# Expert stage: token rows gathered as quarter rows and turned by VectorE, gate and up weights loaded in the matching row order

## The chip, the cores and the metric

The kernel runs on one core of one Trainium2 chip. The metric is the device time in microseconds (us) of one execution. A comparison of two kernels is the ratio of their times.

## The reference

One layer of a decoder block over 1024 tokens of width 1024: a normalised input projection, two attention mixers, a gated merge, an output projection, and then a sparse expert layer. The change touches only the expert layer and the tables that it reads. Cut to that part:

```python
def moe_ffn(h, router_w, router_b, w_gate_up, b_gate_up, w_down, b_down):
    logits = (xf @ router_w + router_b)
    top_logit, top_idx = lax.top_k(logits, TOP_K)          # 4 of 32 experts for each token
    gate = jax.nn.softmax(top_logit, axis=-1)
    ...
    def expert_block(args):                                # x_blk: the rows of one expert
        x_blk, e = args
        gu = x_blk @ w_gate_up[e] + b_gate_up[e]           # 1024 -> 2048
        g = jnp.minimum(gu[:, :D_FF], SWIGLU_LIMIT)
        u = jnp.clip(gu[:, D_FF:], -SWIGLU_LIMIT, SWIGLU_LIMIT)
        act = (u + 1.0) * (g * jax.nn.sigmoid(SWIGLU_ALPHA * g))
        return act @ w_down[e] + b_down[e]                 # 1024 -> 1024
    ...
    out = out.at[buf_token].add(yb * buf_gate[:, None])
```

An expert has 8 MB (8.39 million bytes) of gate and up weights and 4 MB (4.19 million bytes) of down weights in float32, and there are 32 experts.

## The kernel before

The front part (to about 822 us) does the norm, the attention, the merge, the output projection and the routing. Then `experts` runs one block for each of the 32 experts. A block holds up to 160 token rows (`CAP`): 128 rows in the main part, which every block computes, and 32 more (`CAP2`) in the "rest" part, which PE computes only for an expert with more than 128 tokens. Of the 32 blocks 18 have the rest part.

**Weights.** An expert's weights are 12 slabs of 1 MB (128 partitions x 2048 floats, tile `raw`, called `ex_raw` in the profile). Slabs 0 to 7 are gate and up (`load_gate_up`, L1360), slabs 8 to 11 are down (L1988). Each slab comes in two loads of 512 KB, all issued in order by SyncE (SP). The slot of slab i is loaded for the next expert as soon as PE has used it (`raw_mm`), so loads run up to twelve slabs ahead. The biases come in four loads of three rows of 6144 bytes each (L2004). The first four slabs of expert 0 are loaded during routing, from `output_and_route`; the rest of them wait in the program for the first gathered rows (`x_in`).

**Splitting.** For each slab ACT writes a rounded copy `w_hi` (`split_hi`, L2027), DVE the remainder `w_lo` (`split_lo`, L2302), and PE multiplies three times: x_hi by w_hi, x_lo by w_hi, x_hi by w_lo (`gate_up` L2433, `down` L2477). The rest part multiplies the 32 further rows by the raw slab (L2455, L2494).

**Token rows.** GpSimd (POOL) gathers the 128 main rows of the next block but one into `xg` in one indirect DMA of 4 KB rows, and the further 32 rows as quarter rows (piece q of row r stands on partition 32q + r) into `xg2` in a second one (L2137, L2140). PE turns them with ten 128x128 transposes in `turn_x` (L2385), into the PSUM tiles `gu` and `tr`; ACT copies them to `x_hi` and `x_rest` (L2066), DVE writes `x_lo` (L2343). In the program of PE `turn_x(b + 1)` stands in block b between `turn_hidden(b, 1)` (L2393), which turns the second half of the hidden activations, and the down slab 10, whose first matmul waits for ACT's copy `h_hi` of what `turn_hidden(b, 1)` wrote.

**Activation.** For each half ACT writes sigmoid(1.702 g) (L2033), and DVE does three steps: clamp of up (L2312), gate times sigmoid (L2315), minimum and product (L2317). The rest part does the same on 256 columns (L2039, L2325 to L2328).

**Order.** Everything is written out by hand: each engine's order is the order of the code, and engines wait for one another by counting semaphores. SP's queue is in program order. Before the routing it writes `rt_blank` (59 rows of 1280 bytes) to `slots` (L1447) and two tiles of zeros (128 rows of 2560 bytes each) to `xn_s` (L1452). At the end of routing it issues four loads of gate and up weights for expert 0 and then the last store of `xn_s` (the normalised rows, L1467), on which the first gather of the expert stage waits.

Of the kernel before, what the change touches and what calls it, by code (L numbers as in the profile page):

```python
# [21 lines left out]
P = 128  # L22
T = 1024
# [22 lines left out]
NBLK = NE + MAXOVER  # L46

# [1323 lines left out]
def output_and_route(nc, x, w_out, ffn_norm_w, router_w, router_b, ident, nhalf, mT_hi, mT_lo, raw,  # L1371
                     raw_in, wo_hi, wo_lo, out, xn_s, slots, rt, w_gate_up, slab_raw, slab_in, acc, xn_last):
    with ExitStack() as ctx:
# [36 lines left out]
        place, spare_row, quarter = rt["place"], rt["spare_row"], rt["quarter"]  # L1410
        which = rt["which"].rearrange("p (t j) -> p t j", j=TOPK)
# [20 lines left out]
        with nc.Block() as block:  # L1432
# [41 lines left out]
            def _(act):  # L1474
# [49 lines left out]
                act.preload_act_table_set("sigmoid_and_others")  # L1524
# [4 lines left out]
            def _(pool):  # L1529
# [44 lines left out]
                for g in range(Q):  # L1574
# [5 lines left out]
                                        .to_broadcast([P, KD, NE]), ALU.mult).then_inc(c_set, 1)  # L1580
                each = lambda b: b.rearrange("p (j o) -> p j o", o=1).to_broadcast([P, TOPK, NE])
# [294 lines left out]
def experts(nc, xn_s, w_gate_up, w_down, ident, rt, slots, bp_s, out, raw, w_in_, xn_last):  # L1876
# [5 lines left out]
    with ExitStack() as ctx:  # L1882
# [12 lines left out]
        over_n, cum, base1 = (sb(f"ex_{n}", [P, NE]) for n in ("over", "cum", "base1"))  # L1895
        home, low, destf = (sb(f"ex_{n}", [P, NT * TOPK]) for n in ("home", "low", "destf"))
# [4 lines left out]
        idx2 = sb("ex_idx2", [P, 1], U32)  # L1901
# [5 lines left out]
        xg = sb("ex_xg", [P, D])  # L1907
        xg2 = sb("ex_xg2", [P, XW])
# [5 lines left out]
        hid = sb("ex_hid", [P, FF])  # L1914
        hid2 = sb("ex_hid2", [P, 2, P])
# [22 lines left out]
        x_tr, xh_d, xl_d = sem("e_x_tr"), sem("e_xh"), sem("e_xl")  # L1938
        y_ev, y2_ev = sem("e_y_ev"), sem("e_y2_ev")
        idx_in, idx2_d, x_in, y_out = sem("idx_in"), sem("idx2_d"), sem("x_in"), sem("e_y_out")  # L1940
# [36 lines left out]

        block = ctx.enter_context(nc.Block())

        @block.sync  # L1980
        def _(sp):
# [25 lines left out]
            sp.wait_ge(x_in, 32)  # L2007
# [12 lines left out]
        def _(act):  # L2020
# [8 lines left out]
            def sigmoid(b, half):  # L2029
# [5 lines left out]
            def sigmoid_rest(b):  # L2035
# [4 lines left out]
                                     ACT.Sigmoid, scale=ALPHA).then_inc(sg2_d, 1)  # L2040
# [13 lines left out]
            def take_x(b):  # L2054

                if not isinstance(b, int) or b > 0:
                    act.wait_ge(slab_mm, SLABS * (b - 1) + 8 + RING)
                    act.wait_ge(raw_mm, SLABS * (b - 1) + 8)
                for g in range(3):
                    act.wait_ge(x_tr, 3 * b + g + 1)  # L2060
                    if g < 2:
                        dst, src = x_hi[:, 4 * g:4 * g + 4, :], gu[:, 0, g, :].rearrange("p (k c) -> p k c", k=4)
                    else:
                        dst = x_rest[:, :, :].rearrange("p (q h) c -> p h q c", h=2)
                        src = tr[:, 0:2 * P].rearrange("p (h q c) -> p h q c", h=2, q=Q)
                    nc.scalar.activation(dst, src, ACT.Copy).then_inc(xh_d, 1)  # L2066
# [20 lines left out]
            def body(b, over, first=False):  # L2087
# [5 lines left out]
                sigmoid(b, 0)  # L2093
# [5 lines left out]
                sigmoid(b, 1)  # L2099
                sigmoid_rest(b)  # L2100
# [15 lines left out]
        def _(pool):  # L2116
# [14 lines left out]
            def rows():  # L2131

                nc.gpsimd.tensor_scalar(idx2[:, :], nxt[:, 1, 0:1].bitcast(U32), float(Q), quarter[:, 0:1],
# [493 lines left out]
```

## Time and profile before

| | us |
|---|---|
| three runs of the kernel | 2211.8, 2210.14, 2206.59 (median 2210.14) |
| span of the profiled execution | 2210.2 |
| expert stage, from the first instructions to the end | 822 to 2210 |
| a block without the rest part | 35.4 |
| a block with the rest part | 47.5 |

The profile is one execution of the program, and its span is taken as that execution's own time; it is equal to the median of the runs to 0.1 us. Times inside it are us from the start of the span. PE is TensorE's matmuls, PEld its weight loads, DVE VectorE, ACT ScalarE, POOL GpSimd, SP SyncE. There are 16 DMA engines; a DMA share of 1 means that all 16 had a packet under way all the time, and packets that overlap on an engine can bring it above 1.

### The profile page before, as it was taken

The page shows a single profiled execution, that of the slowest core. Times are in us where ns is not written, and L with a number is a line of the kernel's source. Part 1 is how long each engine was busy: PE and PEld are TensorE (multiplying, and loading weights), DVE is VectorE, ACT ScalarE, POOL GpSimd, SP SyncE. Part 2 cuts the span into 40 slices and gives each one's busy share as a digit, 9 for nine tenths or more (in the row PEclk, how much of TensorE's full clock was granted, in tenths as well). Part 3 has the DMA queues.
Part 4 walks back from the last instruction along what each step waited for, and adds up shares of the span by engine and source line. Part 5 has one row for each costly group of instructions (what it writes and reads, how often), then busy time and mean ns, then how long its engine had stood idle before and what let it go on. Part 6 is the DMA issues. An engine that isn't in the chain of part 4 may idle for free.

```text
span 2210.2 us, 39028 instructions
## 1 busy us (share of the span) xinstructions
PE 2131.3 (96%) x13778; PEld 1656.0 (75%) x13779; DVE 1612.0 (73%) x1575; ACT 1323.9 (60%) x1496; POOL 595.1 (27%) x556
## 2 busy tenths in 40 slices
PE   7989999999999978999999999999999999999997
PEld 7867777777777766777777777777887777777775
DVE  4165767676576456888888887898997778777787
ACT  4266666757453225576676675676876566665665
POOL 1120101010075342153354431232341222222222
PEclk9999999999999988999999999999999999999998
DMA  4101212111266539899999998999998889888993
GB/s 153 37 22 47 68 35 70 36 58 59 82 193 198 185 126 334 296 326 340 312 349 340 317 345 291 357 351 343 396 370 318 292 310 321 306 305 267 332 320 117
DMA packets 267125, 515.15 MB, mean 233 GB/s; under 512 B 34821, under 2 KB 77264, under 8 KB 267052
## 3 DMA queue, kind: packets, MB, share of 16 engines
q1 hardware_dynamic: 243052, 471.90, 59.5%
q0 software_dynamic: 17088, 39.14, 7.1%
q10 hardware_dynamic: 6912, 3.15, 0.5%
q8 instruction: 44, 0.72, 0.1%
q14 instruction: 29, 0.24, 0.0%
HBM read 475.82 MB, written 42.45 MB: 234 GB/s over the span
## 4 chain that ended last, share of the span: by engine, by line
PE 58%; SPq 1%; issue 1%; DMA 1%; DVE 1%; ACT 0%; POOL 0%; ACTq 0%; POOLq 0%; DVEq 0%
PE ex_gu L2433 30%; PE ex_yp L2477 15%; PE ex_rest L2455 6%; PE ex_rest L2494 3%; PE ex_gu L2385 1%; SPq L1360 1%; PE ex_tr L2393 1%; PE ex_gu L2393 1%; DMA ex_bias<-bp_s 1%; PE ex_gu L2420 0%; DVE ex_wlo L2302 0%; ACT ex_whi L2027 0%; PE ex_tr L2385 0%; PE ex_yp L2424 0%; PE ex_rest L2449 0%
## 5 line engine op out<-in xcount | busy, mean ns | idle before, releaser
L2302 DVE TENSOR_TENSOR ex_wlo<-ex_raw,ex_whi 128x2048 fp32r<-128x2048 f32 x387 | 873.7, 2289 | 197.5 <-ACT ex_whi L2027 178.0
L2027 ACT ACTIVATE ex_whi<-ex_raw 128x2048 fp32r<-128x2048 f32 x387 | 733.6, 1927 | 181.0 <-PE ex_gu L2433 132.8
L2433 PE MATMUL ex_gu<-ex_whi,ex_xhi 128*128 128x512 f32 x1024 | 284.3, 399 | 5.2 <-issue 5.2
L2433 PE MATMUL ex_gu<-ex_whi,ex_xlo 128*128 128x512 f32 x1024 | 275.0, 390 | 0.0
L2433 PE MATMUL ex_gu<-ex_wlo,ex_xhi 128*128 128x512 f32 x1024 | 274.7, 390 | 0.0
L2433 PEld LDWEIGHTS ex_gu<-ex_whi,ex_xhi 128*128 128x128 f32 x1024 | 186.4, 188 | 61.2 <-issue 26.2
L2433 PEld LDWEIGHTS ex_gu<-ex_whi,ex_xlo 128*128 128x128 f32 x1024 | 192.8, 188 | 41.1
L2433 PEld LDWEIGHTS ex_gu<-ex_wlo,ex_xhi 128*128 128x128 f32 x1024 | 192.8, 188 | 40.8
L57 PE MATMUL at_job<-xnT_hi,at_whi 128*128 128x512 f32 x416 | 179.6, 432 | 5.2 <-DVE at_nxt_qa L777 2.8
L59 PE MATMUL at_job<-xnT_hi,at_wlo 128*128 128x512 f32 x416 | 165.1, 397 | 0.0
L58 PE MATMUL at_job<-xnT_lo,at_whi 128*128 128x512 f32 x416 | 164.6, 396 | 0.0
L741 POOL TENSOR_TENSOR at_wlo<-at_raw,at_whi 128x1024 fp32r<-128x1024 f32 x15 | 36.1, 2405 | 452.1 <-ACT at_whi L554 452.1
L2137 POOL DMA_INDIRECT ex_xg<-xn_s,ex_nxt x33 | 33.8, 1025 | 430.6 <-PE ex_tr L2385 428.8
L2147 POOL DMA_INDIRECT out_dram<-ex_ytok,ex_cur x32 | 68.2, 2132 | 295.5 <-issue 224.7
L2477 PE MATMUL ex_yp<-ex_whi,ex_hhi 128*128 128x512 f32 x512 | 144.8, 404 | 0.0
L2477 PE MATMUL ex_yp<-ex_whi,ex_hlo 128*128 128x512 f32 x512 | 137.5, 390 | 1.2 <-DVE ex_hlo L2335 1.2
L2477 PE MATMUL ex_yp<-ex_wlo,ex_hhi 128*128 128x512 f32 x512 | 137.3, 390 | 0.0
L2455 PE MATMUL ex_rest<-ex_raw,ex_xrest 128*32 128x256 f32 x2304 | 135.7, 381 | 0.0
L2477 PEld LDWEIGHTS ex_yp<-ex_whi,ex_hhi 128*128 128x128 f32 x512 | 90.9, 188 | 30.1 <-issue 7.4
L2477 PEld LDWEIGHTS ex_yp<-ex_whi,ex_hlo 128*128 128x128 f32 x512 | 96.0, 188 | 22.5 <-DVE ex_hlo L2335 1.6
L2477 PEld LDWEIGHTS ex_yp<-ex_wlo,ex_hhi 128*128 128x128 f32 x512 | 96.1, 188 | 20.8
L2455 PEld LDWEIGHTS ex_rest<-ex_raw,ex_xrest 128*32 128x32 f32 x2304 | 70.4, 110 | 53.3 <-issue 12.7
(381 smaller groups left out, 3631.6 us busy)
## 6 DMA issues: line engine op xcount, KB each, us to landing
ex_raw<-in_w_gate_up_dram SPq DMA_DIRECT2D x512, 512.0 KB
ex_raw<-in_w_down_dram SPq DMA_DIRECT2D x256, 512.0 KB
at_raw<-in_w_in_dram SPq DMA_DIRECT2D x25, 512.0 KB
gT<-at_gst SPq DMA_DIRECT2D x32, 256.0 KB, 2.3
mg_g<-gT SPq DMA_DIRECT2D x32, 256.0 KB, 3.8
raw_o<-in_w_out_dram SPq DMA_DIRECT2D x8, 512.0 KB, 5.9
op_x<-in_x_dram SPq DMA_DIRECT2D x8, 512.0 KB, 4.1
out_dram<-op_h SPq DMA_DIRECT2D x8, 512.0 KB, 2.9
```

Source lines behind the costliest of these rows:

```text
L57: nc.tensor.matmul(out, w_hi, x_hi, start=first, stop=False)
L58: nc.tensor.matmul(out, w_hi, x_lo, start=False, stop=False)
L59: return nc.tensor.matmul(out, w_lo, x_hi, start=False, stop=last)
L741: nc.gpsimd.tensor_tensor(w_lo[:, s, :, :], raw[:, s, :, :], w_hi[:, s, :, :].bitcast(F32), ALU.subtract).then_inc(wlo_d, 1)
L2027: nc.scalar.activation(w_hi[:, i % RING, :], raw[:, i % SLABS, :], ACT.Copy).then_inc(hi_d, 1)
L2147: pool.indirect_dma_start(out=out[0, :, :], out_offset=bass.IndirectOffsetOnAxis(ap=cur[:, 0, 0:1].bitcast(U32), axis=0), in_=ytok[:, :], ...
L2302: nc.vector.tensor_tensor(w_lo[:, slot, :], raw[:, i % SLABS, :], w_hi[:, slot, :].bitcast(F32), ALU.subtract).then_inc(lo_d, 1)
L2393: last = nc.tensor.transpose(dst[:, k * P:(k + 1) * P], hid[:, (4 * half + k) * P:(4 * half + k + 1) * P], ident[:, :])
L2433: mm = nc.tensor.matmul(gu[:, half, h, :], x[:, k, :], w[:, kk, h, :], start=half == 0 and k == 0 and n == 0, stop=k == KD - 1 and n == 2)
L2455: mm = nc.tensor.matmul(part(g), x_rest[:, k, :], gate_up_slab(raw, i)[:, kk, :, g * P:(g + 1) * P], start=k == 0, stop=k == KD - 1)
L2477: mm = nc.tensor.matmul(yp[:, nh, :], x[:, k, :], w[:, kk, nh * HALF:(nh + 1) * HALF], start=False, stop=k == KD - 1 and n == 2)
L2494: mm = nc.tensor.matmul(part(g), h_rest[:, k, :], down_slab(raw, i)[:, kk, g * XW:(g + 1) * XW], start=k == 0, stop=k == KD - 1)
```

## The change

**Gather.** `xg` becomes 128 partitions x 5 pieces of 256 floats. Piece a (0 to 4) is gathered by an indirect DMA of its own: quarter rows of the 32 tokens in slots 32a to 32a + 31, with quarter q of token r on partition 32q + r. The row numbers for on-chip blocks are made once before the first block (`rows_of`, by seven more small DVE steps and sixteen small matmuls).

**Turn.** DVE transposes 32x32 blocks (`turn_x`, `turn_x_rest`: two of 128x512 and one of 128x256 per block) from `xg` into `x_t`, which lies in the tile `hid`, and into `x_rest`. ACT's copy to `x_hi` and DVE's `x_lo` read `x_t` in place of PSUM; ACT's copy to `x_rest` goes. PE's `turn_x` is gone.

**Weights' rows.** With this layout partition 32q + r of K tile k holds input channel 256q + 32k + r, where before it was 128k + p. So `load_gate_up` reads the rows of the weights in that order: the source's outermost count is the quarter q (4), then r (32), then the halves and 512 contiguous floats. The destination is as before: 128 partitions, each two runs of 512 floats. The down loads are unchanged.

**Activation.** ACT's function is now gate times sigmoid(1.702 gate) in one (`Gelu_apprx_sigmoid`), so that DVE's L2315 and L2326 go.

```diff
+NQ = CAP // CAP2
...
-    gate_up_v = w_gate_up.rearrange("a e (k p) (h c) -> (a e) p k h c", p=P, h=2)
+    gate_up_v = w_gate_up.rearrange("a e (q k r) (h c) -> (a e) q r k h c", q=Q, k=KD, h=2)
     half, pair_of_k = divmod(i, 4)
     for kk in range(2):
         sp.dma_start(raw[:, i, :].rearrange("p (k h c) -> p k h c", k=2, h=2)[:, kk, :, :],
-                     gate_up_v[bass.ds(e, 1), :, 2 * pair_of_k + kk, :, half * HALF:(half + 1) * HALF]
-                     .rearrange("a p h c -> (a p) h c")).then_inc(raw_in[i], 16)
+                     gate_up_v[bass.ds(e, 1), :, :, 2 * pair_of_k + kk, :, half * HALF:(half + 1) * HALF]
+                     .rearrange("a q r h c -> (a q) r h c")).then_inc(raw_in[i], 16)
...
-                nc.scalar.activation(sg[:, :], gu[:, half, 0, :], ACT.Sigmoid, scale=ALPHA).then_inc(sg_d, 1)
+                nc.scalar.activation(sg[:, :], gu[:, half, 0, :], ACT.Gelu_apprx_sigmoid).then_inc(sg_d, 1)
...
+            def gather(table):
+                for a in range(NQ):
+                    pool.indirect_dma_start(out=xg[:, a, :], out_offset=None, in_=xn_s.rearrange("t (q c) -> (t q) c", q=Q),
+                                            in_offset=bass.IndirectOffsetOnAxis(ap=table(a), axis=0)).then_inc(x_in, 16)
...
-                nc.vector.tensor_tensor(sg[:, :], gu[:, half, 0, :], sg[:, :], ALU.mult).then_inc(part_d, 1)
...
+            def turn_x(b, g):
+
+                if g == 0:
+                    dve.wait_ge(x_in, 16 * NQ * (b + 1))
+                after(dve, h_tr, 3 * b + g - 2)
+                mine = slice(4 * g, 4 * g + 4)
+                nc.vector.transpose(x_t[:, mine, :].rearrange("p k (a c) -> p k a c", a=Q),
+                                    pieces[:, mine, 0:Q, :]).then_inc(x_tr, 1)
...
                 split_lo(b, 11)
+                turn_x(b + 1, 0)
+                turn_x_rest(b + 1)
                 hidden_lo(b, 1)
+                turn_x(b + 1, 1)
                 take_x(b + 1)
...
                 turn_hidden(b, 1, alone=not more)
                 if more:
                     turn_hidden_rest(b)
-                turn_x(b + 1)
                 main(10)
```

The order of PE's instructions in a block, between the down slabs 9 and 10, of the kernel before (`ex_hid` is the hidden tile, `ex_hhi` ACT's copy of its turned form, `e_hh` the count of those copies):

```order
L2477 MATMUL ex_yp<-ex_wlo,ex_hhi 128x512 x3
L2393 MATMUL ex_gu<-ident,ex_hid 128x128 [waits e_hid]
L2393 MATMUL ex_gu<-ident,ex_hid 128x128 x3
L2380 ISA
L2385 MATMUL ex_gu<-ident,ex_xg 128x128 [waits x_in]
L2385 MATMUL ex_gu<-ident,ex_xg 128x128 x7
L2385 MATMUL ex_tr<-ident,ex_xg 128x128 x2
L2463 REGISTER_ALU
L2467 REGISTER_ALU [waits e_hi]
L2477 MATMUL ex_yp<-ex_whi,ex_hhi 128x512 [waits e_hh]
```

The same place in the changed kernel:

```order
L2494 MATMUL ex_yp<-ex_wlo,ex_hhi 128x512 x3
L2410 MATMUL ex_gu<-ident,ex_hid 128x128 [waits e_hid]
L2410 MATMUL ex_gu<-ident,ex_hid 128x128 x3
L2480 REGISTER_ALU
L2484 REGISTER_ALU [waits e_hi]
L2494 MATMUL ex_yp<-ex_whi,ex_hhi 128x512 [waits e_hh]
```

The ten transposes of token rows are gone, so the matmul that waits for ACT's copy stands right behind the transposes that the copy reads.

The order of SP's instructions from the end of routing into the expert stage, which is the same in both kernels but for line numbers, here of the changed one (`op_mm` counts the output projection, `op_xn_d` the normalised rows):

```order
L1361 DMA ex_raw<-in_w_gate_up_dram 128x2x512 [waits op_mm]
L1361 DMA ex_raw<-in_w_gate_up_dram 128x2x512 x3
L1469 DMA xn_s<-op_xn 128x1024 [waits op_xn_d]
L1434 UNCONDITIONAL_BRANCH [waits op_xn_out1,op_h_out1,rt_zout,op_xn_out0,op_h_out0]
L1990 UNCONDITIONAL_BRANCH [waits barrier_Pool_Activation_PE_DVE_SP_release]
L1361 DMA ex_raw<-in_w_gate_up_dram 128x2x512 [waits x_in]
L1361 DMA ex_raw<-in_w_gate_up_dram 128x2x512
L2014 DMA ex_bias<-bp_s 3x3072 [waits e_ones]
```

No instruction moved in this piece; four of the reordered loads stand ahead of the last store of `xn_s`.

## Rows read from the trace of the kernel before

**Rows 1.** The page: DMA busy share in 40 equal slices of the span.

```profile
DMA  4101212111266539899999998999998889888993
```

**Rows 2.** The page: the chain that ended last, by line.

```profile
PE ex_gu L2433 30%; PE ex_yp L2477 15%; PE ex_rest L2455 6%; PE ex_rest L2494 3%; PE ex_gu L2385 1%; SPq L1360 1%; PE ex_tr L2393 1%; PE ex_gu L2393 1%; DMA ex_bias<-bp_s 1%; PE ex_gu L2420 0%; DVE ex_wlo L2302 0%; ACT ex_whi L2027 0%; PE ex_tr L2385 0%; PE ex_yp L2424 0%; PE ex_rest L2449 0%
```

**Rows 3.** Windows, one block with rest, one without: busy by engine, clock, DMA share.

```profile
1471.30:1518.70 47.40, 47.40 (x375) 35.12 (x374) 38.45 (x27) 29.25 (x25) 8.49 (x9) 1.00 0.87 300
1436.00:1471.00 35.00, 35.00 (x168) 28.59 (x167) 33.50 (x25) 27.12 (x24) 13.59 (x9) 1.00 1.04 392
```

**Rows 4.** DMA queues, 837 to 2140 us: packets, MB, share of 16 engines.

```profile
q1 hardware_dynamic: 170535, 390.75, 81.5%
q0 software_dynamic: 15776, 36.15, 11.1%
```

**Rows 5.** DMA, 1438 to 1447 us, inside a block without rest.

```profile
DMA packets 1289, 3.71 MB, mean 412 GB/s; under 512 B 145, under 2 KB 145, under 8 KB 1289
```

**Rows 6.** DMA issues, whole span: KB each.

```profile
ex_raw<-in_w_gate_up_dram SPq DMA_DIRECT2D x512, 512.0 KB
ex_raw<-in_w_down_dram SPq DMA_DIRECT2D x256, 512.0 KB
...
ex_bias<-bp_s SPq DMA_DIRECT2D x128, 18.0 KB
...
slots<-rt_blank SPq DMA_DIRECT2D x1, 73.8 KB
```

**Rows 7.** SP timeline: a store of 59 rows, then two of 128 (start, us).

```profile
717.25 0.29 SPq L1447 DMA_DIRECT2D slots<-rt_blank  x1
717.58 0.81 SPq L1452 DMA_DIRECT2D xn_s<-rt_zeros  x2
```

**Rows 8.** DMA, 716 to 724 us: GB/s in 40 slices of 0.2 us.

```profile
GB/s 138 82 21 3 1 1 1 1 1 2 1 27 263 320 320 326 307 358 320 358 192 128 166 134 102 77 26 26 26 26 26 26 26 26 26 26 0 0 0 0
```

**Rows 9.** DMA, 721.70 to 723.10 us, in the tail of rows 8.

```profile
DMA packets 15, 0.04 MB, mean 26 GB/s; under 512 B 1, under 2 KB 1, under 8 KB 15
```

**Rows 10.** SP timeline, end of routing (start, us, what).

```profile
811.80 2.61 SPq L1360 DMA_DIRECT2D ex_raw<-in_w_gate_up_dram  x4
821.02 0.33 SPq L1467 DMA_DIRECT2D xn_s<-op_xn  x1
829.77 1.21 SPq L1360 DMA_DIRECT2D ex_raw<-in_w_gate_up_dram  x2
```

**Rows 11.** POOL timeline: first gather of the stage.

```profile
824.51 1.25 POOL L2178 DMA_INDIRECT ex_xg<-xn_s,ex_tab  x1 [6.79 <-DVE ex_tab L2248]
```

**Rows 12.** Timeline, end: last matmuls of the program.

```profile
2194.28 1.07 PE L2477 MATMUL ex_yp<-ex_wlo,ex_hhi 128*128 128x512 f32 x4
```

**Rows 13.** PE timeline, four equal matmuls behind idle time, and later.

```profile
841.03 1.71 PE L2433 MATMUL ex_gu<-ex_wlo,ex_xhi 128*128 128x512 f32 x4
...
847.15 1.07 PE L2433 MATMUL ex_gu<-ex_wlo,ex_xhi 128*128 128x512 f32 x4
```

**Rows 14.** Timeline, block without rest: PE's turns and ACT's copy.

```profile
1464.27 0.60 PE L2393 MATMUL ex_gu<-ident,ex_hid 128*128 128x128 f32 x4
1464.70 1.04 PE L2385 MATMUL ex_gu<-ident,ex_xg 128*128 128x128 f32 x8
1464.90 0.60 ACT L2046 ACTIVATE ex_hhi<-ex_gu 128x512 fp32r<-128x512 f32 x1 [3.12 <-PE ex_gu L2393]
...
1465.72 1.18 PE L2477 MATMUL ex_yp<-ex_whi,ex_hhi 128*128 128x512 f32 x4
```

**Rows 15.** The same place in a block with rest.

```profile
1508.23 0.60 ACT L2046 ACTIVATE ex_hhi<-ex_gu 128x512 fp32r<-128x512 f32 x1 [3.92 <-PE ex_gu L2393]
1508.25 1.04 PE L2385 MATMUL ex_gu<-ident,ex_xg 128*128 128x128 f32 x8
...
1509.26 1.17 PE L2477 MATMUL ex_yp<-ex_whi,ex_hhi 128*128 128x512 f32 x4
```

**Rows 16.** Groups of DVE's instructions, 850 to 2210 us: busy us, mean ns.

```profile
L2315 DVE TENSOR_TENSOR ex_sg<-ex_gu,ex_sg 128x512 f32<-128x512 f32 x64 | 43.5, 680 | 0.0
```

More of the change, by code:

```diff
@@ L2057, in take_x @@
                     act.wait_ge(slab_mm, SLABS * (b - 1) + 8 + RING)
[L2058 to L2066, printed above, removed]
+                for g in range(2):
+                    mine = slice(4 * g, 4 * g + 4)
+                    act.wait_ge(x_tr, 2 * b + g + 1)
+                    nc.scalar.activation(x_hi[:, mine, :], x_t[:, mine, :], ACT.Copy).then_inc(xh_d, 1)
             def take_y(b):
@@ L2092, in body @@
                     split_hi(b, i)
-                sigmoid(b, 0)
+                swish(b, 0)
                 split_hi(b, 7)
@@ L2166, in next_rows @@
                     load_slots(b)
-                    hold(pool, idx_in, 16 * (1 + Q) * (b - NE + 1), spare)
-                rows()
-                hold(pool, idx2_d, b + 1, spare)
-                if not isinstance(b, int) or b > 0:
-                    hold(pool, x_tr, 3 * b, spare)
-                gather()
+                    hold(pool, idx_in, 16 * (1 + Q * (1 + NQ)) * (b - NE + 1), spare)
+                    nc.gpsimd.tensor_scalar(idx[:, :], nxt_q[:, :, 0].bitcast(U32), float(Q), quarter[:, 0:1],
+                                            ALU.mult, ALU.add).then_inc(idx_d, 1)
+                hold(pool, idx_d, b, spare)
+                hold(pool, x_tr, 2 * b, spare)
+                hold(pool, xr_tr, b, spare)
+                gather(lambda a: idx[:, a:a + 1])
             def first_rows():
@@ L2314, in activate @@
                 dve.wait_ge(sg_d, n + 1)
-                nc.vector.tensor_tensor(sg[:, :], gu[:, half, 0, :], sg[:, :], ALU.mult).then_inc(part_d, 1)
-                dve.wait_ge(part_d, 6 * b + 2 * half + 2)
+                dve.wait_ge(part_d, 3 * b + half + 1)
                 nc.vector.scalar_tensor_tensor(out=us, in0=sg[:, :], scalar=SWISH_CAP, in1=us, op0=ALU.min, op1=ALU.mult).then_inc(hid_d, 1)
             def activate_rest(b):
-                gate, up = (rest[:, :].rearrange("p (a h c) -> p a h c", a=2, h=2)[:, :, h, :] for h in range(2))
+                up = rest[:, :].rearrange("p (a h c) -> p a h c", a=2, h=2)[:, :, 1, :]
                 dve.wait_ge(sg2_d, b + 1)
@@ L2376, in _ @@
             pe.sem_inc(slab_mm, RING)
-            def turn_x(b):
-                pe.wait_ge(x_in, 32 * b + 32)
-                for g in range(3):
-                    dst = gu[:, 0, g, :] if g < 2 else tr[:, :]
-                    for k in range(4 if g < 2 else 2):
-                        src = xg[:, (4 * g + k) * P:(4 * g + k + 1) * P] if g < 2 else xg2[:, k * P:(k + 1) * P]
-                        last = nc.tensor.transpose(dst[:, k * P:(k + 1) * P], src, ident[:, :])
-                    last.then_inc(x_tr, 1)
             def turn_hidden(b, half, alone=False):
@@ L2528, in _ @@
             for h in range(2):
-                last = nc.tensor.matmul(tr[:, 2 * NE * h:2 * NE * (h + 1)], rt["table"][:, h * P:(h + 1) * P],
-                                        rt["pair_sum"][:, :], start=True, stop=True)
+                nc.tensor.matmul(tr[:, 6 * NE * h:6 * NE * h + 2 * NE], rt["table"][:, h * P:(h + 1) * P],
+                                 rt["pair_sum"][:, :], start=True, stop=True)
+            for a in range(Q):
+                for q in range(Q):
+                    last = nc.tensor.matmul(turned_q[q * CAP2:(q + 1) * CAP2, a, :], rt["table"][:, a * CAP2:(a + 1) * CAP2],
+                                            rt["pair_sum"][:, 0:NE], start=True, stop=True)
             last.then_inc(t_tr, 1)
-            pe.wait_ge(tab_d, 2)
-            turn_x(0)
             def body(b, over):
```

106 lines of the change are left out of this document (61 added, 45 removed).

## The prediction

> **What bounds the kernel now.** I read the page's chain of work first. In the expert stage it is PE nearly throughout: the gate and up matmuls, the down matmuls and the two rest products hold 54% of the span, of the 63% that the stage takes [rows 2]. The windows of single blocks say the same: 35.00 of 35.00 us busy without rest, 47.40 of 47.40 with it, at the full clock (1.00 is 2.4 GHz) [rows 3]. Two others stand close behind. DVE is busy 33.50 of 35.00 us, and the DMA engines have a share of 1.04, that is, no free time in a block without rest; a block with rest leaves them some (0.87) [rows 3]. Over the stage the 16 engines are near their limit in every slice [rows 1], and when they are full they move 412 GB/s [rows 5], which is 25.8 GB/s for one engine. So the kernel stands on two legs: PE's work, and all 16 DMA engines carrying the weights at once. The change takes a little from the first and touches the second.
>
> **The loads of weights, the part that decides.** Bytes, descriptors and destination stay the same, the order of the source's rows does not: the source's outermost count was a run of 128 partitions' rows and is now 4 quarters. The question is over how many of the 16 engines such a transfer is spread. The trace has one transfer that answers half of it. SP issues at 717.25 a store of 59 rows of 1280 bytes (73.8 KB), and behind it two stores of 128 rows [rows 6, 7]. The two spread: the rate is about 320 to 358 GB/s. But then the core moves 26 GB/s and nothing else from 721.2 to 723.2 [rows 8], in packets that come one at a time: 15 in 1.40 us [rows 9]. 26 GB/s is one engine's share of 412. So the 59 rows were all on one engine (59 x 1280 B at 25.8 GB/s is 2.9 us), and what that engine owed of the two stores behind them (2 x 8 rows of 2560 B, 1.6 us) came late. 59 has no divisor up to 16 but 1, while 128 rows go to 16. That is what an even division of the outermost count gives. A source whose outermost count is 4 can be divided so by 4 at most, although the destination has 128. I take it that the reordered loads run on 4 engines. No row shows a transfer whose two sides differ in this way, so this is an inference and keeps a chance against it.
>
> The Trainium skill ("DMA: Bandwidth & Descriptors", section "Why a DMA increments its semaphore by 16 and not by 1") states the same rule outright: the number of engines is the largest up to 16 that divides the slowest dimension of both sides, and on the queue that SP uses it is the lowest-numbered ones. The 59 rows agree with it. By that rule these loads all share the same four engines; with a spread over 16 the sum would be that of the first rival.
>
> Do successive loads take the same four? After the 59 rows the zeros' share on that engine waited, which shows only that an engine's queue is in order. Were the fours rotated, the load would even out and the slowdown vanish; that is part of the first rival.
>
> **The sum for four engines.** What one of the four has to do for one block:
> - Gate and up: 16 loads of 512 KB (512 loads for 32 blocks) [rows 6] are 8.39 MB, a quarter of it 2.10 MB, at 25.8 GB/s 81.3 us.
> - Down: 8 loads, 4.19 MB over 16 engines, 0.262 MB: 10.2 us.
> - Biases: four loads of 18 KB [rows 6] over three engines: 24.6 KB each, 1.0 us.
> - Gathers and stores of POOL's queue: 11.1% of the engines' time from 837 to 2140 [rows 4], 145 us over 30.9 blocks of 42.2 us, 4.7 us. The gathers become five of 128 KB where they were one of 512 KB and one of 128 KB, the same bytes; I leave the term as it is.
>
> Sum 97.2 us for each block, against 35.4 to 47.5 now. It is not hidden: the prefetch is one block deep, and demand exceeds supply in every block. Of block 0 eight of the sixteen gate and up loads were made in routing, so the stage has 31.5 x 81.3 + 32 x 15.9 = 3070 us of work for these four engines.
>
> The start: four loads issued at 811.80 keep them busy 4 x 131 KB / 25.8 GB/s = 20.3 us each, until 833. The last store of `xn_s` stands behind them (issued at 821.02), and the first gather, which runs at 824.51 now, waits for it [rows 10, 11]: about 835. Its rows arrive 5.3 us later (829.77 is where SP goes on now), so streaming begins at 840. The four loads of slabs 0 and 1, early in routing, are done long before they are needed; they delay the loads and stores of routing that are issued behind them by up to 20 us once, which its double buffers mostly cover; I count nothing, at most 15.
>
> The end: behind the last landing stand the split and product of a last slab and perhaps the rest, some 8 us; from the last matmul to the end it is 2210.2 - 2195.4 = 14.9 us [rows 12]. Together 23.
>
> 840 + 3070 + 23 = 3933 us. I add 27 for unevenness (a load that waits because its slot is freed late) and say **3960**.
>
> PE cannot become the bound again, even if its clock falls for want of work. Behind idle time four matmuls take 1.71 us where the same four take 1.07 later [rows 13]. If all of PE's work took twice as long (1.2 against 2.4 GHz), a block with rest would need 95 us, still under 97, and one without 71.
>
> Bounds. Low: if POOL's packets and the weights' overlap as the share of 1.04 suggests, 3070 becomes 2950 and the time 3813. High: over the whole stage the weights' queue moved 390.75 MB in 81.5% of 1303 us on 16 engines [rows 4], 23.0 GB/s for one; all terms at that rate give 31.5 x 91.2 + 32 x 17.2 = 3423 and 4290. So 3780 to 4300.
>
> **The other edits.** They would matter only if the loads were spread over 16.
> - PE's ten transposes start at 1464.70 and the matmul behind them at 1465.72: 1.02 us; with rest 1.01 us [rows 14, 15]. But that matmul needs ACT's copy, which ends at 1465.50, or 1508.83 with rest, and then a weight load (some 0.2 us). Without the transposes PE would wait for ACT until about 1465.7 and 1509.05. The gain is 0 and 0.2 us, 18 x 0.2 = 4 us in all, where adding up transposes gives 33.
> - DVE loses two products of 0.68 us [rows 16] and one of half the columns, and gains transposes of the same three sizes. The trace has no transpose on DVE; from nothing (hidden) to twice a product's time the change per block is -1.8 to +1.8 us. At the pace of the products, the nearest row, it is 0.
> - ACT loses the copy to `x_rest`, off the path; its function costs one pass as before. POOL issues five gathers where it issued two, at some 1.3 us each [rows 11], and has 8.49 to 13.59 us of work in a block [rows 3]. The small steps ahead of block 0 and three more gather issues delay the start by some 3 us.
>
> **The rivals.**
> - *The loads spread over 16 engines after all* (the division looks at the destination only, or the fours rotate), and PE's removed transposes turn into the wait for ACT: 2210 - 4 + 3 to 2210 - 8: 2202 to 2209. For it: the destination's count is 128 and unchanged, and the trace's one odd transfer has 59 on both sides. This is the case that is not slower; it decides as soon as a load gets 16 engines, or if four engines carried over 270 GB/s. 0.11.
> - *Spread, and the transposes come back in full*: 33 x 1.0 us, 2177. Against it the end of ACT's copy [rows 14, 15]. 0.03.
> - *Spread, but a small loss*: a share of 1.04 [rows 3] has no room for more and smaller gather packets, or DVE's transposes cost double and it needs 33.5 + 1.8 = 35.3 us of a block's 35.4. One us for each of 14 blocks without rest and some at the start: 2225 (2216 to 2260). 0.06.
> - *Four engines*: 0.80.
>
> **How the numbers follow.** 0.2% (4 us) is about what a measurement of this kernel can tell from no change. Faster 0.03 and 0.07 of the first rival: 0.10; same 0.04; slower 0.86. The range 3780 to 4300 is that of the likeliest case and leaves out the 0.20 of the others.
>
> **What the profile would show.** Right: mean rate in the stage near 135 GB/s, a DMA share of 0.25 to 0.4; ACT's `split_hi` waits for loads of `ex_raw` and leads the chain; the stage takes about 3100 us, a block 97 whether it has rest or not; PE about 40% busy; the first gather near 835. Wrong: a DMA share near 1 and blocks of 35 us, which would mean that the loads were spread.

## The result and the profile after

The changed kernel takes 4310.31 us (median of 4 runs, 4304.81 to 4316.56), the kernel before 2210.7 us on the same chip; the ratio is 1.951 (95% interval 1.948 to 1.954). Forecast were 3960 us and a range of 3780 to 4300: slower, by the way that was named, and 350 us more than said, 10 us above the range.

The page of the changed kernel, its slices of DMA share and rate, and the queue from which the weights come (packets, MB, share of 16 engines), with the same queue of the kernel before last:

```profile
DMA  3121245343444344444434444443344433444443
GB/s 93 31 60 50 63 124 185 113 132 125 130 127 130 127 129 127 129 126 129 127 125 132 129 127 129 129 131 130 124 128 126 131 123 124 127 127 125 130 126 96
q1 hardware_dynamic: 236908, 471.88, 33.5%
...
q1 hardware_dynamic: 243052, 471.90, 59.5%
```

Where the share was 0.8 to 0.9 [rows 1] it is 0.3 to 0.4, with the same megabytes. The count of packets says over how many engines a load goes, since each engine that takes part ends its share with a packet of 4 bytes (from 2110 to 2120 us, where only gate and up run, there are 485 packets of 2048 bytes, about two loads, and 8 of 4 bytes). The kernel before has 243052 packets in this queue, the changed one 236908. The difference, 6144, is 512 loads times 12: 16 engines before, 4 after.

Windows of the changed kernel: two blocks with rest, one without, and the stretch in which the down loads start (busy by engine, clock, DMA share, GB/s).

```profile
2092.20:2202.10 109.90, 49.78 (x368) 35.78 (x370) 35.07 (x25) 27.98 (x22) 14.32 (x12) 0.72 0.40 126
2202.10:2312.70 110.60, 49.42 (x366) 35.65 (x367) 35.05 (x25) 27.97 (x22) 14.35 (x12) 0.72 0.40 126
2312.70:2418.20 105.50, 39.56 (x158) 30.51 (x158) 34.74 (x25) 28.00 (x22) 15.32 (x12) 0.68 0.41 131
2184.00:2198.00 14.00, 0.00 (x0) 0.00 (x0) 1.92 (x1) 0.00 (x0) 0.00 (x0) 0.50 1.03 243
```

A block takes 105.5 to 110.6 us instead of 35.0 to 47.4 [rows 3]; PE is busy in less than half of it, and more than half of its time is at the lower of its two clock levels (0.50 where it stands idle, 1.2 GHz; 0.68 to 0.72 in the mean of a block). Within a block the rate changes with what is being loaded. DMA from 2110 to 2170, 40 slices of 1.5 us:

```profile
GB/s 100 98 98 100 101 100 98 98 100 101 100 98 161 94 146 108 160 171 152 96 101 100 98 98 102 98 100 98 100 210 238 82 57 87 102 102 98 102 100 98
```

Where only gate and up weights run it is 98 to 101 GB/s, near four times the 25.8 of one engine [rows 5]. The bumps are GpSimd's gathers and stores, which use the idle engines too. The waits of the whole program that matter (us, times, longest), and SP's queue over two blocks:

```profile
PE ex_gu L2437 <- DMA ex_bias<-bp_s: 1839.8, 32, 61.5
ACT ex_whi L2037 <- DMA ex_raw<-in_w_gate_up_dram: 1435.4, 171, 13.4
...
SPq L1361 <- PE ex_rest L2472: 262.7, 17, 17.7
```

```profile
2099.78 78.35 SPq L1361 DMA_DIRECT2D ex_raw<-in_w_gate_up_dram  x16
2178.42 5.45 SPq L1998 DMA_DIRECT2D ex_raw<-in_w_down_dram  x2
2184.24 1.61 SPq L2014 DMA_DIRECT2D ex_bias<-bp_s  x4
2186.03 6.99 SPq L1998 DMA_DIRECT2D ex_raw<-in_w_down_dram  x6
2209.35 79.04 SPq L1361 DMA_DIRECT2D ex_raw<-in_w_gate_up_dram  x16
...
2296.75 6.79 SPq L1998 DMA_DIRECT2D ex_raw<-in_w_down_dram  x6
2304.21 17.36 SPq L1361 DMA_DIRECT2D ex_raw<-in_w_gate_up_dram  x3
```

One row was not in the forecast. PE's largest wait is not for weights but for the biases, at slab 3 of each block: their loads are issued behind all sixteen gate and up loads (2184.24) and land at 2202. In a block with the rest part the products of the further rows with slabs 0 to 3 stand behind slab 3, so only then does PE free these slabs, and SP issues nothing from 2193.0 to 2209.35. From 2204 to 2209 the core moves 76 GB/s. In a block without the rest part PE has freed slabs 0 to 2 before it waits, and SP goes on at once (2304.21); so SP's wait occurs 17 times and not 32.

### The profile page after: what moved, and what is told of

Read it like the earlier page. It is cut to its first block, busy times and chain, and to the rows that moved or that the text cites. A ratio compares the mean times of both kernels' runs of the same rounds, so it can differ in the third digit from the quotient of the medians.

```text
span 4314.7 us, 38630 instructions
## 1 busy us (share of the span) xinstructions
PE 2221.9 (51%) x13480; PEld 1682.9 (39%) x13481; DVE 1628.7 (38%) x1584; ACT 1331.5 (31%) x1463; POOL 708.1 (16%) x701
## 3 DMA queue, kind: packets, MB, share of 16 engines
q1 hardware_dynamic: 236908, 471.88, 33.5%
## 4 chain that ended last, share of the span: by engine, by line
SPq 68%; DMA 7%; PE 5%; issue 3%; POOL 0%; DVE 0%; POOLq 0%; ACT 0%; DVEq 0%; ACTq 0%
SPq L1361 60%; DMA ex_bias<-bp_s 7%; SPq L1998 6%; PE ex_gu L2450 2%; SPq L2014 1%; PE op_acc L58 1%; PE op_acc L59 1%; PE op_acc L60 1%; PE ex_rest L2472 0%; DMA xn_s<-op_xn 0%; PE ex_gu L2437 0%; SPq L2005 0%; POOL ex_xg L2141 0%; PE ex_yp L2441 0%; PE op_tr L1815 0%
## 5 line engine op out<-in xcount | busy, mean ns | idle before, releaser
L2437 PE MATMUL ex_gu<-ex_bias,ex_ones 32*128 32x512 bf16 x128 | 19.7, 602 | 1839.8 <-DMA ex_bias<-bp_s 1839.8
L2141 POOL DMA_INDIRECT ex_xg<-xn_s,ex_idx x165 | 275.5, 1670 | 2119.4 <-DVE ex_hid L2347 1949.0
L2450 PE MATMUL ex_gu<-ex_whi,ex_xhi 128*128 128x512 f32 x1024 | 331.1, 451 | 146.5 <-ACT ex_whi L2037 126.3
L2450 PE MATMUL ex_gu<-ex_whi,ex_xlo 128*128 128x512 f32 x1024 | 312.8, 433 | 0.0
L2450 PEld LDWEIGHTS ex_gu<-ex_whi,ex_xhi 128*128 128x128 f32 x1024 | 209.2, 214 | 228.2 <-ACT ex_whi L2037 133.9
L2315 DVE TENSOR_SCALAR ex_hid<-ex_gu 128x512 f32<-128x512 f32 x64 | 44.0, 688 | 672.3 <-PE ex_gu L2450 672.3
L2450 PE MATMUL ex_gu<-ex_wlo,ex_xhi 128*128 128x512 f32 x1024 | 293.8, 411 | 0.7 <-DVE ex_wlo L2305 0.6
L2043 ACT ACTIVATE ex_sg<-ex_gu 128x512 f32<-128x512 f32 x64 | 38.3, 598 | 779.5 <-PE ex_gu L2450 779.5
L2450 PEld LDWEIGHTS ex_gu<-ex_whi,ex_xlo 128*128 128x128 f32 x1024 | 220.0, 215 | 53.5
L2450 PEld LDWEIGHTS ex_gu<-ex_wlo,ex_xhi 128*128 128x128 f32 x1024 | 207.8, 203 | 51.9 <-DVE ex_wlo L2305 3.2
```

What stands on the lines that cost most here:

```text
L2141: pool.indirect_dma_start(out=xg[:, a, :], out_offset=None, in_=xn_s.rearrange("t (q c) -> (t q) c", q=Q), in_offset=bass.IndirectOffsetOn ...
L2450: mm = nc.tensor.matmul(gu[:, half, h, :], x[:, k, :], w[:, kk, h, :], start=half == 0 and k == 0 and n == 0, stop=k == KD - 1 and n == 2)
```

## The experiments

"The run with old rows" and such names are those of the list here. Ratios are to the kernel before, run on the same chip. A time without an interval is that of a single run; the runs of the kernel before lie between 2202 and 2215 us.

**1. The loads' order alone, in the kernel before.**

```diff
-    gate_up_v = w_gate_up.rearrange("a e (k p) (h c) -> (a e) p k h c", p=P, h=2)
+    gate_up_v = w_gate_up.rearrange("a e (q k r) (h c) -> (a e) q r k h c", q=Q, k=KD, h=2)
```

> The kernel before with one edit: the gate and up weights' rows are loaded in the new order (source's outermost count 4 instead of 128 partitions' rows). The tokens keep the old order of channels, so these products meet other channels than the reference's; the work is the same. Theory A (the order of the loads alone makes the whole loss): about 4300 us, blocks of 105 to 110 us, a mean rate near 128 GB/s. Theory B (the five small gathers, the block transposes of VectorE or the new function share in the loss): clearly below the changed kernel's 4310 us, by more than 20 us.

Measured 4207.81 us. This line makes 2000 of the 2103 us (4310.3 less 2207.65, the kernel before on this chip). The rest, 102 us, comes from the other edits, and most of it only in this slowed state (run 2 has 16 us without it): stretches with gate and up alone move 100 to 104 GB/s here and 98 to 101 in the changed kernel, some 2.3 us of a block, 72 us in all. The other 30 us are not taken apart. Theory B is right for a twentieth of the loss.

**2. The changed kernel with the old order of the loads** (the reverse of that diff).

> The changed kernel with the gate and up weights' rows loaded in the order of before; tokens stay in the new order of channels, so these products meet other channels than the reference's, with the same work. It prices all the other edits together. The forecast's first rival's working says 2202 to 2209 us (transposes' gain 4 to 8 us by way of ScalarE's copy, start 3 us later); if the ten transposes came back in full it would be 2177 us; if the small gathers or VectorE's transposes cost, 2216 to 2260 us. My value is 2205 us.

Measured 2223.61 us, 1.0068 (1.0054 to 1.0082). All other edits together cost 16 us, where my value of 2205 was a gain of 3. From the first bias product of the first block to that of the last it takes 1324.4 us where it was 1319.8. From there to the end it takes 51.8 us where it was 42.2. GpSimd's timeline shows why (start, us; the end was forecast from [rows 12]):

```profile
2192.72 2.46 POOL L2136 DMA_DIRECT2D ex_nxt_q<-slots  x5
2196.64 4.42 POOL L2170 TENSOR_SCALAR ex_idx<-ex_nxt_q,rt_quarter 128x5 uint32<-128x5 uint32 x1 [1.46 <-DMA ex_nxt_q<-slots]
2202.10 2.06 POOL L2141 DMA_INDIRECT ex_xg<-xn_s,ex_idx  x1 [1.04 <-issue]
...
2209.54 1.65 POOL L2148 DMA_INDIRECT out_dram<-ex_ytok,ex_cur  x1 [0.30 <-issue]
2211.49 1.60 POOL L2151 DMA_INDIRECT out_dram<-ex_ytok,ex_piece  x1 [0.30 <-issue]
```

The last two stores stand in GpSimd's queue behind the fetching of a block that does not exist. Before, that was two gathers, issued by 2193.1, and the last store went out at 2201.30; now it is 20 more small loads, an index computation and five gathers.

In the blocks themselves the removed transposes became a wait for ACT's copy:

```profile
1464.48 0.60 PE L2410 MATMUL ex_gu<-ident,ex_hid 128*128 128x128 f32 x4
1465.77 1.21 PE L2494 MATMUL ex_yp<-ex_whi,ex_hhi 128*128 128x512 f32 x4 [0.69 <-ACT ex_hhi L2056]
```

**3. Each load cut into its four quarters of 32 partitions.**

```diff
-    for kk in range(2):
-        sp.dma_start(raw[:, i, :] ... gate_up_v[bass.ds(e, 1), :, :, 2 * pair_of_k + kk, ...])
+    for q in range(Q):
+        mine = raw[q * CAP2:(q + 1) * CAP2, i, :].rearrange("p (k h c) -> p k h c", k=2, h=2)
+        for kk in range(2):
+            sp.dma_start(mine[:, kk, :, :], gate_up_v[bass.ds(e, 1), q, :, 2 * pair_of_k + kk, ...])
```

> The changed kernel, same data and same order of rows, but each load of 512 KB is cut into its four quarters of 32 partitions: the source's outermost count is then 32. By the rule of the forecast (an even division of the outermost count, here 16) each quarter goes over 16 engines. Theory A (the count of 4 is the cause): the rate in the expert stage is back near 400 GB/s, and the time within 2200 to 2300 us; the upper part if SyncE, which must now issue 64 gate and up loads in a block, becomes late (a short issue with room in the ring is not yet priced in this case). Rival (the stride of the rows in the source, or their place in memory, makes the loads slow): it stays above 4000 us. The Trainium skill (DMA: Bandwidth & Descriptors, section Why a DMA increments its semaphore by 16 and not by 1) has the rule of A.

Measured 2817.05 us, 1.2755 (1.2737 to 1.2772): neither theory's time. The queue has 267628 packets, 30720 more than the changed kernel, which is 2048 loads times 16 less 512 times 4. So all engines carry them, as theory A says, but in a stretch with hardly anything but gate and up (1850 to 1870) they move only 222 GB/s:

```profile
DMA packets 2678, 4.43 MB, mean 222 GB/s; under 512 B 540, under 2 KB 540, under 8 KB 2678
```

**4. Biases loaded once** (`load_bias(e)` out of SP's loop, `bias_in` awaited at 32; every block uses expert 0's biases).

> The changed kernel, but the biases are loaded once, for expert 0, and used for every block, so TensorE waits for no bias load in the loop (the output has expert 0's biases in every block). Theory (the bias loads stand in SyncE's queue behind all gate and up loads of their block; TensorE waits for them at slab 3 for some 60 us, frees the first four slots only after they land, and the four engines run dry for 7 to 10 us per block): blocks shrink from 106 to 110 us to 97 to 101 us, all alike, and the time to 3950 to 4050 us. Rival (the engines are slower in themselves than the forecast took them, 84 us for gate and up and 14 us for down, and the gap is only the order in which it shows): the time stays above 4200 us.

Measured 4222.6 us. The wait for biases is gone, and 88 us with it, not 300; behind the first (94.0 us) the blocks take 104 to 107 us with one of 109, not 97 to 101. SP's queue stands full throughout. The theory of the gap is right for 88 us, 2.8 us of a block in the mean; the rest of the error lay in the sizes, as the rival says. Most of the 88 us lies in blocks with the rest part: behind the first they take 109.0 to 111.5 us in the changed kernel, those without 105.5 to 106.9 and one 109.2.

**5. Halves of 64 partitions, new order** (each load in two, outermost count 2).

> The changed kernel with each 512 KB load cut into two halves of 64 partitions, whose source has an outermost count of 2. Theory A (a count of 2 gives two engines, always the same two): gate and up take 2 x 84.3 = 169 us of a block, the rest of these engines' work stays 21 us, a block takes 190 us, the whole 840 + 31.5 x 169 + 32 x 21 + 23 = 6860 us (6700 to 7000). Rival B (successive loads begin at different engines, and the count of engines was not what slowed it): 4310 us or less. Rival C (two engines for each load, but the two halves of a load on different pairs): about 4310.

Measured 6988.6 us; a block takes 189.6 us without and 193.5 with the rest part, and gate and up alone move 49 to 51 GB/s. DMA from 2520 to 2700:

```profile
GB/s 51 52 45 50 50 50 67 107 98 50 50 50 49 50 50 50 50 49 50 50 49 50 50 137 45 51 50 50 49 50 50 49 50 50 50 50 49 50 75 261
```

The queue has 236908 packets again, 1024 loads times 2 where it was 512 times 4. Theory A. B and C are out: successive loads take the same engines. Loads wait behind one another here, so on different engines they would move more than two engines' share.

**6. Down weights loaded once as well** (SP's loop over `range(8)`; every block uses expert 0's down weights).

> The run with the biases loaded once, and the down weights loaded once too, for expert 0 (every block uses expert 0's biases and down weights). Left for the loads are gate and up and GpSimd's gathers and stores. With biases once a block took 105.5 us, of which gate and up take 84.3 us by the rate of the stretches that hold nothing else (8.39 MB at 99.5 GB/s), so 21.2 us are shared by down loads and GpSimd's queue; the forecast had 10.2 and 4.7. Theory D (the down loads are the term that was too small, 15 us or more on the loaded engines): a block takes 89 to 91 us, the whole 3690 to 3760 us. Theory G (the down loads take 10.2 us as forecast, GpSimd's many small transfers 11 us): a block takes 95 us and the whole 3880 us.

Measured 3713.03 us, a block 88.9 us. The down loads cost (4222.6 - 3713.0) / 31 = 16.4 us of a block, forecast 10.2. What is left, 88.9 - 84.3 = 4.6 us, is put down to GpSimd's queue, forecast 4.7. Theory D.

**7. Quarters of 32 neighbouring partitions with the old order of rows.**

> Quarter loads as in the run that cuts each load into four quarters of 32 partitions, but with the weights' rows in the order of before (products meet other channels than the reference's, the work is the same). In the run with quarter loads the core moved 220 GB/s at a DMA share of 0.9, and a packet of 2048 bytes took 131 ns in the mean instead of 91. Theory P (32 neighbouring partitions take only about half of what the engines can write, whatever the source): again 2800 us and some 220 GB/s. Rival Q (the order of rows in the source is slow to read): back at about 2230 us. The Trainium skill (SBUF - State Buffer, section on the DMA port swizzle) puts 32 neighbouring partitions on half of the ports, which is P.

Measured 2820.51 us, the same as 2817. The order in the source is out as the reason.

**8. Quarters of every fourth partition** (old order; the source's rows are then every fourth, too).

```diff
-        mine = raw[q * CAP2:(q + 1) * CAP2, i, :].rearrange("p (k h c) -> p k h c", k=2, h=2)
+        mine = raw[bass.ds(q, CAP2, Q), i, :].rearrange("p (k h c) -> p k h c", k=2, h=2)
```

> The same again, but a quarter is every fourth partition instead of 32 neighbouring ones: same size, number and packets of the loads, same rows in all (products meet other channels than the reference's). Theory P (which partitions are written decides): the rate is back near 330 GB/s or more and the time within 2220 to 2300 us. Rival R (128 KB loads are slow in themselves, by their number: 64 instead of 16 for gate and up in a block): stays near 2800 us.

Measured 2851.56 us. By what I had written, theory P was dead. But the time alone misled: two limits lie at the same height here. DMA from 1860 to 1880, and SP's queue in the same run:

```profile
q1 hardware_dynamic: 2399, 3.95, 64.2%
```

```profile
1853.26 50.95 SPq L1363 DMA_DIRECT2D ex_raw<-in_w_gate_up_dram  x64
1904.45 0.91 SPq L2001 DMA_DIRECT2D ex_raw<-in_w_down_dram  x2
```

The engines are idle for a third of the time, and in this block, one without the rest part, SP never stops: 64 issues in 50.95 us, 0.80 us each, which with the down and bias loads behind them fill the block's 57 us. The packets of 2048 bytes are quick again (84 ns at the median over the stage, 134 with neighbouring partitions; medians of the packets' own times in the traces). With neighbouring partitions SP needed 48.5 us for its 64, too, 0.76 each: SP's issues alone would hold the quarters near this time in both runs, and what the partitions do had to be seen with fewer loads. Bytes do not set this price: a down load of 512 KB takes 0.46 us to issue here (0.91 for 2).

**9. Quarters in the order 0, 2, 1, 3.**

> The run with quarter loads of the new order (which computes the reference), with the quarters issued in the order 0, 2, 1, 3 instead of 0, 1, 2, 3. If partitions below 64 and above share their halves of the ports, loads of both kinds are then nearer to each other in each engine's queue. Theory (engines drift apart by more than one load, so both halves are written at once): clearly under 2817 us, at best near 2250. Rival (all engines stay within one load of each other): 2817 us, within 1%.

Measured 2786.27 us, 1.1% less: nearly the rival's, and after run 8 it says little, since SP needs 48.5 us for 64 issues here as well.

**10, 11. Loads of 256 KB, 32 in a block, cut by 64 partitions or by columns** (old order; the diff leads from the first to the second).

```diff
-        for g in range(2):
-            sp.dma_start(raw[64 * g:64 * (g + 1), i, :] ... [:, kk, :, :], ...)
+        for h in range(2):
+            sp.dma_start(raw[:, i, :] ... [:, kk, h, :], ...)
```

> Loads in the order of before, each of 512 KB cut into two of 64 partitions (256 KB), all over 16 engines (products meet other channels than the reference's, the work is the same). For quarters the stretches with gate and up alone moved 222 GB/s, 0.59 us for 128 KB where 412 GB/s would need 0.32: 0.27 us for each load beyond its bytes. Theory (a fixed price of 0.27 us for each load on all engines): 32 gate and up loads in a block take 32 x 0.91 = 29 us, with down and the rest 44 to 47 us for a block without rest where 35.6 are needed for TensorE; the whole 2350 to 2480 us. Rival (the price comes only with very small loads, 4 packets for each engine): within 2223 to 2260 us.

> Loads in the order of before, each of 512 KB cut into two of 256 KB, not by partitions but into the gate's and the up's columns: 128 partitions of 2 KB each (products meet other channels than the reference's, the work is the same). Size, number and packets are those of the run with halves of 64 partitions, which moved 250 GB/s in stretches with gate and up alone, at 145 ns for a packet of 2048 bytes. Theory R (loads of 256 KB are slow by their size and number): 2611 us again. Theory P (what is slow is that the 16 engines write 64, or 32, or every fourth of the partitions at a time, and share something there two by two): back within 2223 to 2260 us, near 400 GB/s in those stretches.

Measured 2610.93 us and 2226.69 us, with 251244 packets in both. The DMA of the run by partitions, 1850 to 1870:

```profile
DMA  9999999999999999999999999999999999999999
...
DMA packets 2547, 4.72 MB, mean 236 GB/s; under 512 B 282, under 2 KB 282, under 8 KB 2547
```

The engines have no free time and move 236 GB/s, little over half of the 412 of [rows 5]. By columns SP issues its 32 loads in 24.19 us (0.76 each, below the block's 35) and the kernel runs as with whole loads. Its rate from 1862 to 1880, gate and up alone:

```profile
GB/s 346 346 373 382 332 378 373 332 250 319 382 414 387 428 387 419 396 401 387 410 355 328 219 87 14 0 0 0 82 182 291 228 278 259 337 319 300 255 291 282
```

Until the loads run out that is 370 GB/s in the mean, and a packet of 2048 bytes takes 84 ns at the median, 142 by partitions (1850 to 1870). Size and number are equal, so the partitions written at one time make the difference: theory P, for 64 neighbouring ones. One rival is only argued against: with the partitions the rows that a load reads change, too, and no run parts the two; that the order of rows changed nothing in run 7 speaks for the writing side. The Trainium skill ("SBUF — State Buffer", section "Door 1: The DMA port swizzle") says that partitions reach only 8 of 16 ports if bit 6 of their number is the same. These runs agree (236 of 412 GB/s, and quick packets with every fourth partition in run 8); its ports themselves show in no row.

**12, 13, 14. Three steps to a kernel that is not slower.** The loads get their old order back, and the tokens' channels are put into the matching order where they are normalised; then the transposes of the hidden values move forward; last, GpSimd fetches for a further block only if there is one.

```diff
+                    for q in range(Q):
+                        mine = lambda b: b.rearrange("p (k q r) -> p k q r", k=KD, q=Q)[:, :, q, :]
+                        last = nc.vector.scalar_tensor_tensor(
+                            out=xn[:, s, q * XW:(q + 1) * XW].rearrange("p (k r) -> p k r", k=KD),
+                            in0=mine(ht[:, s, :]), scalar=rstd[:, t:t + 1], in1=mine(wB[:, :]), ...)
...
-                main(9)
-                turn_hidden(b, 1, alone=not more)
+                main(9, between=lambda: turn_hidden(b, 1, alone=not more))
...
-                next_rows(b + 2, on_chip=not over and (not isinstance(b, int) or b + 2 < NE))
+                if not (isinstance(b, int) and b == NE - 1) and not over:
+                    next_rows(b + 2, on_chip=not isinstance(b, int) or b + 2 < NE)
```

> The changed kernel with the weights' rows in the order of before, and the tokens' channels put into the matching order where VectorE normalises them (its one product per tile of 128 tokens is cut into four that write 32-element runs), so that the reference is computed again. The gathers in quarters, VectorE's block transposes and the new function stay. Theory: the loads go over 16 engines again and the time is that of the run with old rows, 2223 us, plus at most some us for four products instead of one in routing: 2222 to 2230. Rival (the run with old rows was fast only because its data were unmatched): above 2300.

> As the run with the turned normalisation, and TensorE does the four transposes of the second half of the hidden values (and those of the rest) after the first 8 of the 12 products of down slab 9 instead of behind all 12, so that ScalarE's copy is done when slab 10 comes. Theory (the removed token transposes turned into a wait for that copy, 18.0 us in 32 blocks): 16 to 18 us less than the turned normalisation alone, 2205 to 2209. Rival (VectorE, ScalarE or the weights' loads, all close to the block's 35 us, take over as the bound, so that the gain shows only in blocks with rest): 8 to 10 us less.

> As the run before in this list, and the last blocks of GpSimd's queue put in another order: the row indices and the five gathers for a further block, which nobody needs unless an expert overflows, are issued only if there is such a block, no longer ahead of the last two stores. In the run with old rows the last store was issued at 2211.49 us where it was 2201.30 before, behind 20 small loads, an index computation of 4.42 us and five gathers. Theory (that queue makes the end 9.6 us longer): 9 to 11 us less than without it, 2195 to 2199. Rival (the end waits for TensorE, ScalarE or the landing of the stores): within 2 us of the run without it.

Measured 2224.49 us (1.0078, 1.0063 to 1.0093), 2211.29 us (1.0013, 1.0002 to 1.0024) and 2201.3 us (0.9971, 0.9958 to 0.9984). The first is as expected. The second gives 13 us more, between theory and rival: blocks with rest went from 47.3 to 46.6 us, blocks without from 35.6 to 35.5 only, because a wait for VectorE, 14 times, took the place of ScalarE's, as the waits of that run show:

```profile
PE ex_yp L2500 <- DVE ex_hlo L2340: 8.7, 14, 2.0
```

The third gives 10 us at the end, as expected; its last store is issued at 2189.24, behind the other store of the same result and nothing else. This kernel is 6 us (0.3%) faster than the kernel before.

## Why the prediction was off by 350 us

What bounds the kernel was right. What failed are sizes in the sum for four engines: above all the down loads, put at 10.2 us of a block where they cost 16.4, then the rate for gate and up, and the biases, whose wait was not in the sum.

- **What bounds the kernel, and how many engines.** Right. Four engines carry each load (packet counts), always the same (98 to 101 GB/s with loads waiting behind one another; run 5 for two), and this one line makes 2000 of the 2100 us (runs 1, 2). I had given this case 0.80.
- **Gate and up, 81.3 us of a block.** Mis-sized: 84.3 us (8.39 MB at 98 to 101 GB/s), 3.0 x 31.5 = 95 us. I took one engine's rate from full stretches of all sixteen; with the other edits undone the rate is some 2.5% higher (run 1), and a packet of 2048 bytes takes 84 ns where it takes 86 in the changed kernel. Which of them costs it was not tried.
- **Down, 10.2 us.** The largest error: 16.4 us (run 6), 6.2 x 32 = 198 us. The 10.2 holds for down loads by themselves: the 412 GB/s of [rows 5] are mostly theirs. I took them to go at that rate beside gate and up, and missed what happens while all engines do down loads and four of them still do gate and up. DMA of the changed kernel, 2186 to 2194, and of the kernel before, 1466 to 1470, both with the two kinds side by side:

```profile
DMA packets 611, 1.86 MB, mean 233 GB/s; under 512 B 48, under 2 KB 48, under 8 KB 611
...
q1 hardware_dynamic: 611, 1.86, 104.7%
```

```profile
DMA packets 625, 1.68 MB, mean 421 GB/s; under 512 B 52, under 2 KB 52, under 8 KB 625
```

  All engines are full in both, and each packet takes nearly twice as long after the change: 160 ns at the median for 2048 bytes where it is 85 just before (2180 to 2184), 287 for 4096 bytes where it is 160 behind, when gate and up have ended (2201 to 2205). In the kernel before it is 84 and 159 with the two side by side. This lasts some 12 us of each block, and meanwhile the four engines get on at half their pace, which loses some 6 us, what the term was short of. It fits what run 10 shows, if each of the four now writes the 32 neighbouring partitions of its quarter, but no run tests this cause by itself.
- **GpSimd's queue, 4.7 us.** Right as far as shown: run 6 leaves 4.6 for it, although the gathers are five now.
- **27 us for unevenness, and 1.0 for biases.** I looked for loads whose slots are freed late and overlooked why they would be: PE waits for the biases, which stand behind all gate and up loads of their block in SP's queue. It costs 88 us in all (run 4), 2.8 us of a block in the mean, against 27 and 31.5 in the sum: 30 us short.
- **The sum.** 95 + 198 + 30 = 323 of the 350 us. Of the other 27, 5 are the start, since SP goes on with gate and up at 844.63 where I had streaming from 840, and 10 the end: in run 4, without the wait for biases, the last packet of weights ends at 4187.3 and the span at 4220.9, 33.6 us where I had 23. The remaining 12 stay open. The first block is long (146.8 us from its bias product to the next, block 1 then 109.7), but that is the wait for biases again: without it, it takes 94.0.
- **The bounds.** The low end let packets overlap by the share of 1.04; the time went the other way. The high end used the mean rate of the queue over the stage, 23.0 GB/s for an engine, for all terms. That is too slow for gate and up (24.9) and too fast for down in this mixture, 0.262 MB in 16.4 us: that it came within 20 us of the result is luck, by errors that cancel.
- **The signs.** First gather near 835: 836.64. Mean rate 135, share 0.25 to 0.4: 126 to 131, 0.40. PE 40% busy: 37 to 45% in these windows. A block 97 us with or without rest: wrong in both, 110 and 105.5. ScalarE's `split_hi` leads: only half right; it waits 1435 us, but PE's wait for biases is longer (1840).
- **The removed transposes, 0 and 0.2 us.** Right in kind: PE waits 0.69 and 0.47 us where it had worked 1.0. But four products now start 0.916 us after the four before them, not 0.906, at the same granted clock of 1.00, and blocks without rest took 35.6 us against 35.4. This too was not in the forecast.
- **The rival "spread, but a small loss", 2225 us.** Run 2 gives 2223.6, so the number stood, but its reasons did not: neither DVE's transposes (0.69 us, like its products) nor the share of 1.04 made it. The fetching at the end of GpSimd's queue did, 9.6 us; I had priced its issues ahead of block 0 only. Another 4.6 us came in the blocks: most of it in three of them, in one of which PE waits 2.4 us for biases; those with rest got 0.2 us shorter, those without 0.2 longer.

## What to carry to other kernels

Before a source pattern is reordered, look at the outermost count on both sides of the transfer, since it can set how many engines carry it; if the order is needed, make it where an engine writes the data anyway (here the normalisation), not in the pattern of a large load. When an engine set becomes the bound, don't price its transfers by rates from stretches with another pattern (here they held alone and failed where two kinds overlapped), and look in each queue for the small thing that stands behind the large ones and holds the consumer. Work for "the next block" at the end of a queue is free until it stands ahead of the last store.

## What the runs showed that I had not expected

- An issue on SP's queue takes 0.76 to 0.80 us for a gate or up load, whether of 128 or 256 KB: 64 in a block of 35 us cannot be had from one queue (24.19 us for 32, 48.5 for 64).
- Loads that write 64 neighbouring partitions at a time move 236 GB/s with all 16 engines busy, those that write 128 up to 412.
- While four engines work off the reordered loads and all sixteen the down loads, the core moves 233 GB/s with all engines busy; the same two kinds of load side by side move 421 GB/s in the kernel before.
- At the same granted clock PE's products came 1% further apart in every kernel with the other edits (0.916 and 0.906 us for four), and not in run 1, which has only the new order of loads. It is 0.916 at the mean 74 GB/s of run 5 as at the some 320 of run 2, so the amount of DMA traffic is not what does it; the cause stays open.
